# Grid attention: the context keys' products first in a step, with a signal of their own for VectorE's first maximum

## The reference, cut to what matters

```
GRID_W = 64
CTX_LEN = 256
C_HEADS = 16
C_KH = 8
C_KW = 16
```

## Time and profile before

| what | value |
|---|---|
| median of 3 runs | 2403.13 us (2402.93 to 2406.48) |
| profiled execution, own time | 2404.68 us |
| profiled execution, span of the trace | 2403.0 us |
| mean granted TensorE clock | 0.977 |
| PE busy | 2280.4 us (95%) |
| DVE busy | 1279.4 us (53%) |
| ACT busy | 926.8 us (39%) |

### The profile page before, as it was taken

One profiled execution on the slowest core, in us unless ns is written; L12 is line 12 of the kernel. 1 busy time (PEld: TensorE's weight loads), 2 busy tenths in 40 slices (PEclk: granted clock), 3 DMA queues, 4 the chain that ended last, 5 costly groups with the idle time before them and its releaser, 6 DMA issues.

```text
span 2403.0 us, 32270 instructions
## 1 busy us (share of the span) xinstructions
PE 2280.4 (95%) x13137; PEld 1851.5 (77%) x13137; DVE 1279.4 (53%) x1864; ACT 926.8 (39%) x1555; POOL 261.9 (11%) x167
## 2 busy tenths in 40 slices
PE   6998999999999998899999999998999989998988
PEld 6776678888888765688888878896676878887776
DVE  5678348873225677359853155225555363126764
ACT  3446642222224355642222232324544242115653
POOL 2001112121001011122121000000000000001220
PEclk9999999999999998999999999999999999999999
DMA  5210015632333200035522311321000124223311
GB/s 153 90 60 1 1 53 192 195 121 88 105 97 102 63 35 1 19 123 176 190 91 89 121 63 50 104 78 47 17 12 14 56 71 138 70 70 56 61 30 53
DMA packets 144612, 189.48 MB, mean 79 GB/s; under 512 B 41141, under 2 KB 94402, under 8 KB 144450
## 3 DMA queue, kind: packets, MB, share of 16 engines
q1 hardware_dynamic: 108816, 168.26, 21.5%
q10 hardware_dynamic: 35586, 19.01, 3.5%
q0 software_dynamic: 64, 0.16, 0.0%
HBM read 179.94 MB, written 7.47 MB: 78 GB/s over the span
## 4 chain that ended last, share of the span: by engine, by line
PE 81%; DVE 11%; issue 3%; ACT 3%; ACTq 1%; POOL 0%; DMA 0%; DVEq 0%; POOLq 0%
PE ps L487 63%; PE ps L1720 3%; PE ps L2257 2%; PE ps L1759 2%; DVE ps L1911 2%; PE ps L1724 2%; DVE score L2143 1%; DVE probs_t L1941 1%; PE ps L1773 1%; DVE top L2140 1%; PE ps L2286 1%; PE ps L2274 1%; PE ps L675 1%; ACT probs L1825 1%; DVE sink_part L1901 1%
## 5 line engine op out<-in xcount | busy, mean ns | idle before, releaser
L463 DVE TENSOR_TENSOR w_low<-w_raw,w_high 128x2048 fp32r<-128x2048 f32 (+4 forms) x140 | 305.3, 2181 | 519.6 <-ACT w_high L458 519.6
L458 ACT ACTIVATE w_high<-w_raw 128x2048 fp32r<-128x2048 f32 (+4 forms) x140 | 253.0, 1807 | 631.3 <-PE ps L487 616.9
L487 PE MATMUL ps<-h_hi,w_high 128*128 128x512 f32 x976 | 372.3, 381 | 3.4 <-DVE h_lo L2634 3.2
L487 PE MATMUL ps<-h_lo,w_high 128*128 128x512 f32 x976 | 369.8, 379 | 0.0
L487 PE MATMUL ps<-h_hi,w_low 128*128 128x512 f32 x976 | 369.6, 379 | 0.0
L487 PE MATMUL ps<-w_high,h_hi 128*128 128x512 f32 (+3 forms) x736 | 277.8, 377 | 9.3 <-DVE w_low L463 5.9
L487 PE MATMUL ps<-w_low,h_hi 128*128 128x512 f32 (+3 forms) x736 | 274.8, 373 | 0.0
L487 PE MATMUL ps<-w_high,h_lo 128*128 128x512 f32 (+3 forms) x736 | 274.7, 373 | 0.0
L487 PEld LDWEIGHTS ps<-h_hi,w_high 128*128 128x128 f32 x976 | 184.2, 189 | 38.6 <-issue 4.1
L487 PEld LDWEIGHTS ps<-h_hi,w_low 128*128 128x128 f32 x976 | 184.0, 189 | 34.9
L487 PEld LDWEIGHTS ps<-h_lo,w_high 128*128 128x128 f32 x976 | 184.3, 189 | 34.2 <-issue 0.5
(11 more groups left out here) (324 smaller groups left out, 3724.9 us busy)
## 6 DMA issues: line engine op xcount, KB each, us to landing
w_raw<-in_w_gate_up SPq DMA_DIRECT2D x44, 1024.0 KB, 5.2
ada_w<-in_ada_w SPq DMA_DIRECT2D x24, 1024.0 KB, 5.2
w_raw<-in_w_down SPq DMA_DIRECT2D x20, 1024.0 KB, 4.9
w_raw<-in_w_in SPq DMA_DIRECT2D x16, 1024.0 KB, 5.1
w_raw<-in_c_in_w SPq DMA_DIRECT2D x16, 1024.0 KB, 5.5
w_raw<-in_w_out SPq DMA_DIRECT2D x8, 1024.0 KB, 4.8
w_raw<-in_ab_in_w SPq DMA_DIRECT2D x8, 1024.0 KB, 5.1
bias<-bias_scratch ACTq DMA_DIRECT2D x32, 224.0 KB, 5.1
```

What stands on the lines that cost most here:

```text
L458: e.activation(w_high[j % 2][:, 0:size], w_raw[j % 2][:, 0:size], ACT.Copy).then_inc(sig.w_high_done, 1)
L463: e.tensor_tensor(w_low[j % 2][:, 0:size], w_raw[j % 2][:, 0:size], w_high[j % 2][:, 0:size].bitcast(F32), ALU.subtract).then_inc(sig.w_lo ...
L487: mm = e.matmul(dst, lhs, rhs, start=start and a == 0, stop=stop and a == 2)
```

## The change

The order of a step's twelve products is rewritten, so that the six context products come ahead of five of the six products with local keys that followed or surrounded them. A new semaphore, context_scored, is raised by the third T0 product, when both context regions are complete. VectorE's reduction over them waits for context_scored in place of scores_ready, and the wait for scores_ready moves behind it, ahead of the first fused instruction. No instruction is added or removed on any engine.

```
-            ORDER = (("H0", 0), ("T1", 0), ("T1", 1), ("H0", 1), ("T1", 2), ("H1", 0), ("H0", 2), ("H1", 1), ("T0", 0), ("H1", 2), ("T0", 1), ("T0", 2))
+            ORDER = (("T1", 0), ("H0", 0), ("T1", 1), ("T1", 2), ("T0", 0), ("H1", 0), ("T0", 1), ("T0", 2), ("H0", 1), ("H1", 1), ("H0", 2), ("H1", 2))
...
                             if where == "T1" and n == 2:
                                 mm.then_inc(sig.half_scored, 1)
+                            if where == "T0" and n == 2:
+                                mm.then_inc(sig.context_scored, 1)
...
                 def maxima(s):
...
-                    e.wait_ge(sig.scores_ready, B["scores_ready"] + s + 1)
                     if not self.grid:
+                        e.wait_ge(sig.scores_ready, B["scores_ready"] + s + 1)
...
                     b = self.base(s)
+                    e.wait_ge(sig.context_scored, B["context_scored"] + s + 1)
                     ch.step(e.tensor_reduce(out=seed2[:, two], in_=flat[:, b + 512:b + 1024].rearrange("p (m n) -> p m n", m=2),
                                             op=ALU.max, axis=AX.X))
                     if j == 0:
                         e.wait_ge(sig.bias_masked, B["bias_masked"] + u)
+                    e.wait_ge(sig.scores_ready, B["scores_ready"] + s + 1)
                     ch.wait(e)
```

More of the change, by code:

```diff
@@ L422, in build_program @@
         sig.half_scored = semaphore("half_scored")
+        sig.context_scored = semaphore("context_scored")
         sig.sink_ready = semaphore("sink_ready")
@@ L1647, in __init__ @@
                 if grid:
-                    self.counts.update({"qk_high": T, "bias_load0": 64 * (U // 2 - 1), "bias_load1": 64 * (U // 2), "bias_masked": U - 1, "max_ready": 2 * N})
+                    self.counts.update({"qk_high": T, "context_scored": N, "bias_load0": 64 * (U // 2 - 1), "bias_load1": 64 * (U // 2), "bias_masked": U - 1, "max_ready": 2 * N})
                 else:
@@ L3001, in build_program @@
             "tensor": ["ada_done", "bank_done", "sum_step", "qk_bank", "scores_ready", "probs_turned", "o_ready", "gates_summed",
-                       "x_turned", "idx_turned", "idx_scores", "inverse_wide", "fold_ready", "pair_summed", "pair_wide", "half_scored"],
+                       "x_turned", "idx_turned", "idx_scores", "inverse_wide", "fold_ready", "pair_summed", "pair_wide", "half_scored", "context_scored"],
             "gpsimd": ["sq_added", "silu_scaled", "staged_ready", "bias_masked", "pool_prep", "o_scaled", "pair_squared", "pair_staged", "rope_staged"],
```

## The result

The changed kernel took 2408.57 us (median of 22 runs, 2404.23 to 2413.73), the kernel before 2404.93 us in the runs beside it (22 runs, 2396.39 to 2407.49). The ratio, taken over all runs and not of the two medians (which would give 1.0015), is 1.0020, with a 95% interval of 1.0013 to 1.0028, or 3.1 to 6.7 us: slower, about at the 0.2% that the prediction named as the least that can be told. The prediction said 2403.9 within 2398.5 to 2408.5, most likely no change. Its sum was +0.8 us; measured are +3.6 us between the medians, and +2.6 us in the stage between the first trace of each kernel.

The account below looks back on a forecast made before the run. The prediction took VectorE's loop to set the pace, with PE's just below. Full units +0.7, last unit +0.2 - 0.24 + 0.35, first -0.2 made +0.8 us on 2403.13: 2403.9, range 2398.5 to 2408.5.

Parts of the forecast that it names:

- the two loops: VectorE's loop through products, reduction and copy sets 5.02 us in k1 and k2; PE's own floor lies below at 4.69.
- The signal and the block: In each step, the early signal starts the reduction 0.12 us sooner, while PE's block of products grows by 0.35 us.
- the two last steps 4.90: In the last unit, without pieces to turn, the two steps behind k0 each become 0.12 us shorter.
- Rivals 1 to 5: Alternative signal or product-block costs, giving 2399.6, 2397.8, 2407.2, about 2414 and 2400.8 us; chances 0.12, 0.07, 0.10, 0.07, 0.04.
- rival 3: T0's signal costs the upper bound: load at 0.79, no reduction gain, block +0.47, about +4 us (2407.2); chance 0.10.
- The failed step: In k0, the later of PE's 5.20 and VectorE's 4.88 us sets the step, so 5.20 against 5.00 before.
- One of the prediction's own signs: In the profile after, L1725's load wait for VectorE's copy all but goes in k0 to k2, stays in k3.
- the wait for scores_ready costs nothing: Behind VectorE's reduction, the moved wait adds 0: reduction and chained wait take about 0.88, products complete about 0.45 after T0.
- the ends: Outside the six full units: first unit about -0.2 us; last unit k0 +0.20, two steps -0.12 each, last turn_probs +0.35.
- The level: Starting time for the whole kernel: the +0.8 us was put on the runs' median of 2403.13, giving 2403.9.

Follow-up runs that it names:

- bias_wait_first: Changed kernel with VectorE's wait for bias_masked moved ahead of the reduction; 2407.17 us, ratio to the kernel before 1.0008.
- no_inverse: Changed kernel without the grid stage's inverse sums (reciprocal, spreading copy and their wait), so output there isn't normalised; 2407.63 us, ratio to the kernel before 1.0004.
- filled: Changed kernel with the second H0 and first H1 product moved ahead of the first T0 product; 2404.01 us, ratio to the kernel before 0.9994.
- filled_bias_first: Changed kernel with two local products ahead of the first T0 product and the bias_masked wait ahead of the reduction; 2404.63 us, ratio to before 0.9997.
- order_only: Kernel before with the new product order alone, the reduction still waiting for scores_ready; 2417.35 us, ratio to the kernel before 1.0050.
- before_again: Kernel before, unedited, as a kernel of its own; ratio to the kernel before 1.0005.

## Why the prediction was wrong

**What bounds the kernel, and the two loops: right.** PE's floor of 4.69 us a step with 0.32 of slack was real: in k1 and k2 PE now goes on 0.07 before the modelled end of its values, and 5.04 was forecast, 5.05 measured.

**The signal and the block: right.** The waiting product at 0.67 (measured 0.68), the reduction at 1.32 (1.33), the next load at 1.68 (1.69), k3 5.24 (5.22), the two last steps 4.90 (4.88 and 4.89). The load that carries a wait was indeed not done ahead: T0's first product began with its load at 0.68, and the next of its half came 0.22 later, in place of 0.12, while a load without a wait stands 0.12 ahead of its matmul (2203.59, then 2203.71). The Trainium skill (TensorE: Matmul & The Clock Gate, Engine queue depths) says that PE can pull weight loads ahead of matmuls in flight; the trace shows it for the loads that carry no wait, and not for the one that waits, as the rows of before said. Rivals 1 to 5 all fall by these rows. The measured time lies nearest to that of rival 3 (2407.2), but by chance: its load would have come at 0.79 and its reduction at 1.44.

**The failed step** is the line "k0: PE 4.85 + 0.35 = 5.20, VectorE 5.00 - 0.12 = 4.88: 5.20". VectorE's side was worked out as in the other steps, only with the earlier reduction. But in k0 the reduction isn't the first in VectorE's queue: the reciprocal stands ahead of it and waits for the last exponentials, and these hang from turn_probs, which the same prediction had just moved 0.35 later. The same seam in the kernel before:

```profile
2213.51 0.22 ACT L1825 ACTIVATION_READ_ACCUMULATOR probs<-ps,neg_max 128x1 f32 x1
...
2213.77 0.20 DVE L1929 RECIPROCAL sums_inv<-sums 128x8 f32<-128x8 f32 x1 [0.70 <-ACT probs L1825]
2214.08 0.43 DVE L1934 COPY inv_stage<-sums_inv 128x512 f32<-128x512 f32 x1
2214.56 0.69 DVE L1901 TENSOR_REDUCE sink_part<-ps 128x2 f32<-128x512 f32 x1
```

The exponentials end at 2213.73. With the 0.69 that the trace after has from there to the reduction (2214.18, then 2214.87), this second path would have let the reduction start at 2214.42; the products let it start at 2214.56. So the path stood only 0.14 behind the products, and no wait showed it. The sum that was missing: the exponentials ended 5.98 after k3's start before (5.36 + 0.62), the new ones 5.98 + 0.35 = 6.33; k3 takes 5.24; so they end 1.09 into k0, and with 0.69 the reduction starts at 1.78, measured 1.79. VectorE's k0 would then have read 4.88 + 1.78 - 1.32 = 5.34, over PE's 5.20; 5.34 is what bias_wait_first measured. no_inverse shows it as cause: with the reciprocal and its wait gone, k0 is 5.20, exactly the bound that had been named, and the unit 20.51 against the forecast 20.52. The k0 behind the long k3 shows the same. One of the prediction's own signs had failed with this step: the load's wait for the copy, which was to all but go in k0 to k2, went in k1 and k2 and stayed behind k0:

```profile
2218.53 0.19 PEld L1725 LDWEIGHTS ps<-k_high,q_high 64*128 64x128 f32 x2 [0.42 <-DVE probs_t L1946]
```

**Added to it, the third wait**: "the wait for scores_ready costs nothing" held in k1 to k3, not in k0, where the fused instruction already had two waits. 0.11 us, shown by bias_wait_first. Together they make 5.45 in place of 5.20, +0.25 us in five k0 steps; +0.18 in the first, whose reduction starts 1.71 in; nothing in the one behind the long k3. That is +1.4 us.

**A single step** (the 20th, a k3) took 5.57 in place of 5.22 in the changed kernel, +0.35. In all its traces, and in filled, filled_bias_first and bias_wait_first, this same step is long; in before, order_only and no_inverse it isn't. In it VectorE's first fused instruction starts 1.22 behind the reduction and not 0.87:

```profile
2271.49 0.69 DVE L1905 TENSOR_REDUCE sink_part<-ps 128x2 f32<-128x512 f32 x1 [0.88 <-PE ps L1725]
2272.71 0.76 DVE L1916 CUSTOM_DVE_ANT_0 ps<-ps,bias,sink_part 128x512 f32<-128x512 f32 x1 [0.53 <-DVE sink_part L1905]
```

What delays it isn't settled. Since the k0 behind it falls from 5.45 to 5.20, its net cost is 0.10 us.

The account of the stage: forecast +0.8, k0 +1.4, the one step +0.35, makes 2.6; the first traces of the two kernels differ by 2.6, the means of four traces (175.35) and of three (172.90, without before_again's) by 2.45. So the ends came as forecast too: the first unit -0.16 (about -0.2), the part behind the last scores +0.40 (+0.35).

**Outside of the stage.** Some 1 us lies between these 2.6 us and the 3.3 to 3.6 between the medians, and 1 to 2 us up to the two ratios (4.8 and 3.8 us). It isn't settled. The first 22 runs of the changed kernel had a mean granted clock of 0.9759, the 27 of before in the next series 0.9771 (the changed kernel in that same series: 0.9762); at the same clock of 0.977 ten runs of the changed kernel (both series) average 2407.2 and 14 of before 2405.6. A longer stretch at the low clock right behind the stage goes with 0.6 us, and one of the four traces of the changed kernel has it. Whether the change makes it more frequent, these traces can't say.

**The level** was a part of the miss: the forecast started from 2403.13, the median of three runs, and 22 runs gave 2404.93. From there the same +0.8 would have given 2405.7, 2.8 us under the measured time: 1.8 of it in the stage, as told, the rest outside. The time lay 0.07 us above the range.

## What to carry to other kernels

To signal a part of a block early, ask what the new order leaves uncovered: here a wait of PE for itself came directly behind its cause, and two products put between them turned a loss into a small gain in the stage. When a block on one engine grows, follow every consumer of what stands behind it, up to the queue where it meets the path that was made shorter; a path that ends just ahead of another today shows no wait of its own. And give the steps at a seam a sum of their own, with all that stands in each queue there.

## What the runs showed of the hardware that wasn't expected

- A third wait on one instruction of VectorE cost 0.11 us (0.97 against 0.85 from the reduction's start to the fused instruction's). The second costs nothing that shows: 0.88 with one wait (k1 to k3 of the kernel before), 0.86 with two (its k0).
- A weight load that waits for PE's own matmul starts 0.06 after the modelled end of that matmul (2203.15 + 0.28, then 2203.49), and the next product of its half comes 0.22 later instead of 0.12.
- Nearly all steps of a kind between the first and the last unit repeat to 0.02 us, while the whole program moves over some 12 us from run to run. Stretches at 1.2 GHz, most of them far ahead of the changed stage, go with that: among the 27 runs of before, those at a mean clock of 0.979 averaged 2401.4 us and those at 0.975 2407.0.
